# First expert tile in four feature steps: pick, gate product, up product, and half-slot loads

## The chip, the cores and the metric

One core of a Trainium2 chip runs the kernel. The metric is the device time of one execution in microseconds, here the median of several runs. Engines: PE (TensorE), DVE (VectorE), ACT (ScalarE), POOL (GpSimd), SP (SyncE, which here only issues loads).

## What is computed

One decoder layer over 512 tokens of width 2048 in float32: a norm, an input projection, three mixers (attention, S5, HGRN2), an output projection, then a mixture of experts and a final norm. The change lies in the mixture of experts. Cut to what matters:

```
gl = x @ w_group;  g_idx = argmax(gl)                    # 1 of 4 groups
top_vals, top_idx = top_k(el_of_group, 2)                # 2 of 8 experts in it
xs = tokens ordered by expert
h = silu(xs @ w_gate[e]) * (xs @ w_up[e])                # 2048 -> 512
y = h @ w_down[e]                                        # 512 -> 2048
out[token] += gate * y
```

There are 32 experts. Each has 4.2 MB of gate, 4.2 MB of up and 4.2 MB of down weights (float32), and every expert's weights are read once.

## The kernel before, in words

**Tiles and owners.** The experts are worked off in 14 tiles of 128 rows. In a tile the PE array's four column groups of 32 rows each belong to one or more experts. Tile 0 has two experts (`THREE_ONE`: expert 0, fixed at build time, has three groups; the "partner", known only after routing, has one), tile 1 has four (`FOUR`), tiles 2 to 8 two each, tiles 9 to 12 two each, the last one four.

**Parts and slots.** Weights come in parts of 2 MiB (128 partitions x 4096 values): gate half 0, gate half 1, up half 0, up half 1, two for down. Eight slots in SBUF take them. `part` (L783 on) waits until the slot's last reader is done (`slot_used`), then SP issues the load; SP is one queue in order, so a part that waits holds back every part behind it. For tile 0 the parts are numbered 0 to 11 (`fixed_parts`), even ones of expert 0 and odd ones of the partner. Parts 0, 1 are gate half 0; 2, 3 up half 0; 4, 5 gate half 1; 6, 7 up half 1; 8 to 11 down. The partner's parts 5, 7, 9, 11 share their slots with parts 0, 1, 2, 3: part 5 follows part 0, part 7 follows part 1, part 9 follows part 2, part 11 follows part 3. They are loaded in two pieces of 1 MiB: `first_half` (L789) when PE has read the first half of the slot (`half_read`), and `second_half` (L795) when it has read the whole slot (`slot_used`). The order on SP (L831 to L835) is: first pieces of 5 and 7, second pieces of 5 and 7, first pieces of 9 and 11, second pieces of 9 and 11, then tile 1's 24 parts. Tile 1's parts 0 to 3 (gate half 0 of its four experts) go into the slots of tile 0's parts 4, 5, 6 and 7; its parts 4 to 7 go into the slots of tile 0's down parts.

**Tile 0 on PE.** Its rows are picked by products with a 0/1 matrix (`select`): for each quarter f of the features (512 of 2048), 16 products into one bank, which DVE then scales into SBUF (`turned`, one operation each, signalled by `xT_free`). `expert_tile(0, ..., first=True)` does select(0), select(1), then the gate and up products of the first 1024 features (`first_products` with `FIRST_ORDER`: gate half 0, up half 0, gate half 1, up half 1), with the routing's last product `id` between the first two and select(2), select(3) before the third. Each of these four products is 32 calls, 64 instructions in the trace (a call in float32 is two instructions). Before select(0) stands `keep_warm(TURN_BANK[0], 1)` (L1437), one product whose result nobody reads.

**DVE meanwhile** works off the routing: it makes the matrix for `select` (`first_sel`), the order of the experts (`order_ready`, for which SP waits before it can load the partner's parts), the places (`places_ready`, for `id`), then from the result of `id` the token numbers (`slots_ready`), on which POOL gathers tile 1's token rows, 1 MiB, on a DMA queue of its own. `turned` for quarters 0, 1 and for 2, 3 stands at fixed places in this program.

**The other tiles.** `first_products` for tiles 1 on waits for the four `turned` of its tile and for its parts; then come the transposes for the next tile, `hidden_back` and the down products.

## Time and profile before

| | us |
|---|---|
| runs | 1895.19, 1898.34, 1899.38 |
| median | 1898.34 |
| profiled execution | 1895.62 |
| its span in the trace | 1893.8 |
| PE busy | 1773.5 (94%) |
| HBM read | 496.92 MB |
| GB/s in the 40 slices, slices 20 to 39 | 371 to 427 |

The span is the time between the first and the last recorded instruction. A window of the trace gives for a stretch how long each engine was busy, the TensorE clock that was granted (1.00 is 2.4 GHz, 0.50 is 1.2 GHz) and the bytes that the 16 DMA engines moved. A timeline gives instructions in order. "Idle before" is the time in which an engine did nothing ahead of an instruction, with what ended it. The duration of a DMA instruction in SP's timeline is the time to issue it, not to move the data; the list of DMA issues gives the time to landing.

### The profile page before, as it was taken

The numbers are of one execution on the slowest core, as the hardware profiler recorded it, in microseconds if no ns is written. First come the engines' busy times: TensorE is split into PE (matmuls) and PEld (weight loads), VectorE is DVE, ScalarE is ACT, GpSimd is POOL, SyncE is SP. The second block draws the span as 40 slices with busy tenths as digits, with TensorE's granted clock in tenths as the row PEclk, the third lists the DMA queues.
The fourth block names the chain that finished last, engine by engine and source line by source line (L and its number), as shares of the span: only waits on it lengthen the run. The fifth ranks groups of instructions, "written<-read, shape, count | busy, mean of one in ns | idle before, by whom it ended". The sixth has DMA issues, their size and how long they took to land.

```text
span 1893.8 us, 30543 instructions
## 1 busy us (share of the span) xinstructions
PE 1773.5 (94%) x12903; PEld 1088.4 (57%) x12903; DVE 750.8 (40%) x1422; ACT 242.7 (13%) x581; POOL 181.0 (10%) x207
## 2 busy tenths in 40 slices
PE   6999999999999989999987599999999999999985
PEld 4888899878997878888532133332333333333321
DVE  7666685366457543332511112231222322232311
ACT  4012211200325330000100000000000000000021
POOL 1453342000000000000010000000000000000001
PEclk9999999999999999999998799999999999999988
DMA  6343333322112155221989999999999999999997
GB/s 224 104 140 91 101 91 93 100 91 64 60 63 78 51 211 198 73 88 47 374 371 427 426 426 425 425 426 425 426 425 426 426 426 425 426 426 426 419 415 320
DMA packets 67464, 505.74 MB, mean 267 GB/s; under 512 B 18712, under 2 KB 18988, under 8 KB 37688
## 3 DMA queue, kind: packets, MB, share of 16 engines
q1 hardware_dynamic: 47666, 475.85, 62.0%
q0 software_dynamic: 5728, 19.56, 3.0%
q10 hardware_dynamic: 13936, 8.36, 1.8%
q8 instruction: 108, 1.77, 0.4%
q14 instruction: 26, 0.20, 0.0%
HBM read 496.92 MB, written 14.04 MB: 270 GB/s over the span
## 4 chain that ended last, share of the span: by engine, by line
PE 72%; DMA 20%; DVE 3%; ACT 1%; issue 1%; SPq 1%; POOLq 0%; DVEq 0%; ACTq 0%
PE psum L1509 18%; PE psum L1151 16%; DMA arena<-in_moe_w_gate 14%; PE psum L1148 10%; PE psum L1117 10%; PE psum L1465 6%; PE psum L1550 4%; DMA arena<-in_moe_w_up 3%; DMA arena<-in_moe_w_down 2%; PE psum L1217 1%; DVE arena L1978 1%; PE psum L1445 1%; SPq L873 1%; PE psum L1357 1%; DVE arena L1981 1%
## 5 line engine op out<-in xcount | busy, mean ns | idle before, releaser
L1509 PE MATMUL psum<-arena 128*32 128x512 f32 x3584 | 417.7, 620 | 50.5 <-DMA arena<-in_moe_w_gate 21.3
L1978 DVE TENSOR_TENSOR arena<-psum,arena 128x512 f32<-128x512 f32 (+3 forms) x299 | 197.9, 677 | 390.9 <-PE psum L1465 355.5
L1151 PE MATMUL psum<-arena 128*128 128x256 f32 x1456 | 323.2, 381 | 1.2 <-DVE arena L1978 1.2
L1509 PEld LDWEIGHTS psum<-arena 128*32 128x32 f32 x3584 | 119.6, 114 | 340.0 <-issue 335.3
L1151 PEld LDWEIGHTS psum<-arena 128*128 128x128 f32 x1456 | 273.8, 190 | 39.1 <-issue 2.1
L1978 DVE TENSOR_TENSOR arena<-arena,psum 128x256 f32<-128x256 f32 (+1 forms) x143 | 70.4, 492 | 410.3 <-PE psum L1117 124.1
L1148 PE MATMUL psum<-arena 128*128 128x128 f32 x1792 | 205.1, 276 | 0.0
L1148 PEld LDWEIGHTS psum<-arena 128*128 128x128 f32 x1792 | 202.2, 192 | 1.3 <-issue 0.8
L1550 PE MATMUL psum<-arena 128*32 128x512 f32 x1664 | 185.8, 605 | 16.8 <-DMA arena<-in_moe_w_down 16.8
L1117 PE MATMUL psum<-arena 128*128 128x256 f32 x896 | 198.3, 381 | 0.5 <-issue 0.5
L1465 PE MATMUL psum<-arena 128*128 128x512 f32 x416 | 193.6, 609 | 2.3 <-issue 2.3
L1978 DVE TENSOR_TENSOR arena<-arena 128x128 f32<-128x128 f32 (+17 forms) x434 | 175.4, 447 | 31.8 <-ACT arena L1691 24.1
L1117 PEld LDWEIGHTS psum<-arena 128*128 128x128 f32 x896 | 169.4, 191 | 29.2 <-issue 7.3
L1465 PEld LDWEIGHTS psum<-arena 128*128 128x128 f32 x416 | 75.6, 191 | 120.9 <-issue 120.9
L1550 PEld LDWEIGHTS psum<-arena 128*32 128x32 f32 x1664 | 54.3, 112 | 139.0 <-issue 138.0
L656 DVE TENSOR_TENSOR arena<-arena 128x1024 f32<-128x1024 f32 x84 | 109.4, 1302 | 2.3 <-DVE arena L1978 1.1
L1015 POOL TENSOR_SCALAR arena<-arena 128x512 f32<-128x512 f32 x13 | 27.1, 2082 | 727.4 <-PE psum L1465 727.0
L1903 ACT ACTIVATE arena<-psum 128x512 f32<-128x512 f32 x14 | 8.4, 597 | 361.2 <-PE psum L1486 361.2
L1772 ACT ACTIVATE arena<-psum 128x256 f32<-128x256 f32 (+1 forms) x46 | 18.4, 399 | 265.4 <-PE psum L1151 177.5
L1899 ACT ACTIVATE arena<-psum,arena 128x512 f32<-128x512 f32 x14 | 9.6, 687 | 293.6 <-PE psum L1509 227.7
L2621 DVE COPY arena<-psum 128x512 f32<-128x512 f32 x13 | 9.0, 692 | 96.2 <-PE psum L1550 96.2
L2618 DVE COPY arena<-psum 128x512 f32<-128x512 f32 x13 | 9.0, 692 | 85.9 <-PE psum L1550 85.9
(249 smaller groups left out, 1079.4 us busy)
## 6 DMA issues: line engine op xcount, KB each, us to landing
arena<-in_moe_w_gate SPq DMA_DIRECT2D x63, 2048.0 KB, 26.0
arena<-in_moe_w_up SPq DMA_DIRECT2D x63, 2048.0 KB, 24.7
arena<-in_moe_w_down SPq DMA_DIRECT2D x54, 2048.0 KB, 26.5
arena<-in_w_in SPq DMA_DIRECT2D x86, 512.0 KB, 4.6
arena<-in_w_out SPq DMA_DIRECT2D x16, 1024.0 KB, 5.7
arena<-in_moe_w_down SPq DMA_DIRECT2D x12, 1024.0 KB, 15.5
arena<-in_x SPq DMA_DIRECT2D x8, 1024.0 KB, 12.7
arena<-in_moe_w_down SPq DMA_DIRECT2D x16, 512.0 KB, 12.1
```

The lines of the kernel that those rows point to most:

```text
L656: e.tensor_tensor(F(o, BLK), F(a, BLK), F(b, BLK), ALU.subtract).then_inc(sums_ready, 1)
L873: sp.dma_start(dst, src).then_inc(tail_in[p], 16)
L1015: g.tensor_scalar(F(SEL, S), F(IOTA, S), F(SELP, 1), F(SELP + 1, 1), ALU.is_equal, ALU.mult).then_inc(sel_ready, 1)
L1117: last = mm(B(bank, [(1, 2 * P)], off=2 * t * P), F(a + t * P, P), F(w + 2 * i * P, 2 * P), start=(n < 4 and i == 0 and t == 0), stop=(i = ...
L1148: last = mm(B(bank, [(1, P)], off=t * P), F(a + t * P, P), F(w + i * P, P), start=start and t == 0, stop=(i == KH - 1), skip_group_check=True)
L1151: last = mm(B(bank, [(1, HB)]), F(w + i * P, P), F(a, HB), start=start, stop=(i == KH - 1), skip_group_check=True)
L1217: last = mm(B(bank, [(1, S)]), F(w + k * P, P), F(ZT + k * S, S), start=(k == 0), stop=(k == NB5 - 1))
L1357: last = mm(B(bank, [(1, n)]), F(AQ + h * S + i * P, P, m * QK, QK), F(AK + h * S, n, m * QK, QK), start=True, stop=True)
L1465: mm(B(4 + q, [(1, 512)]), F(SEL + t * P, P), F(YSB + q * 512, 512), start=True, stop=True).then_inc(comb_full, 1)
L1509: last = mm(B(bank, [(1, FE)], 32 * g, 32), F(xt + c * CAP + 32 * g, 32), F(SLOT[slot] + (c % 8) * FE, FE), start=(c == 0), stop=(c == KD ...
L1550: last = mm(B(4 + q, [(1, 512)], 32 * g, 32), F(HTE + m * CAP + 32 * g, 32), down_block(slot, m, q), start=(m == 0), stop=(m == FT2 - 1))
L1978: return v.tensor_tensor(o, a, b, op)
```

## The change

Tile 0 gets its own function, `first_tile`. For each quarter f of the features it does select(f), (for f = 1 also `id`), waits for that quarter's `turned`, and does the gate product and the up product of the quarter's 4 chunks. `half_read` is now raised four times: after gate and up of quarter 0, and after gate and up of quarter 2. On SP the orders for parts 5, 7, 9 and 11 stay. New is that tile 1's parts 0 to 3 are loaded in two pieces as well: first pieces when `half_read` reaches 3 (parts 0, 1) and 4 (parts 2, 3), each also behind the landing of the load before it on the same semaphore `half_in`; second pieces when the slot is read. On DVE `turned(0, (0,))` moves behind the place computation, and `turned(0, (1,))` from there to just ahead of the copy of `id`'s result. The `keep_warm` ahead of the picks is gone.

```diff
--- before.py
+++ after.py
@@ -834,9 +834,12 @@
                 for j in two_:
                     second_half(partner, fixed_parts()[j], *FIRST_ORDER[j // 2])
             four, parts = [], four_parts()
-            for j in range(FOUR_L):
-                if j < 4:
-                    four.append(expert(2 + j))
+            for j in range(4):
+                four.append(expert(2 + j))
+                first_half(four[j], parts[j], 0, 0, 3 + j // 2, j % 2)
+            for j in range(4):
+                second_half(four[j], parts[j], 0, 0)
+            for j in range(4, FOUR_L):
                 part(four[j % 4], parts[j], j // 8, j // 4 % 2)
             two_, parts = [expert(6 + i) for i in range(2)], second_parts()
             for j in range(PAIR_L):
@@ -1434,7 +1437,6 @@
 
             for bank in range(8):
                 pe.wait_ge(free[bank], uses[bank] - (bank == use[("id",)][0]))
-            keep_warm(TURN_BANK[0], 1)
 
             def select(fs):
 
@@ -1445,13 +1447,6 @@
                             last = mm(B(TURN_BANK[f], [(1, CAP)], off=c * CAP), F(H0 + t * D + (4 * f + c) * P, P),
                                       F(SB[0] + t * P, P), start=(t == 0), stop=(t == TB - 1))
                     last.then_inc(xT_full, 1)
-
-            def during_first(half):
-
-                if half == 1:
-                    do(("id",))
-                elif half == 2:
-                    select((2, 3))
 
             def combine(m, t):
 
@@ -1486,48 +1481,67 @@
                     last = tr(B(2, [(1, CAP)], off=m * CAP), F(SIL + m * P, P), ident)
                 last.then_inc(hT_full, 1)
 
-            def first_products(n, parts, owner, later, ahead=None, xt=XT):
+            def first_products(n, parts, owner, split):
 
                 ne = max(owner) + 1
-                if xt == XT:
-                    pe.wait_ge(xT_free, 4 * n + 4)
-                for step, (which, half) in enumerate((FIRST_ORDER if xt != XT else ORDER)[:4]):
+                pe.wait_ge(xT_free, 4 * n + 4)
+                if split:
+                    for s in half_in:
+                        pe.wait_ge(s, 16 * 4)
+                for step, (which, half) in enumerate(ORDER[:4]):
                     bank = 2 + which
                     here = parts[step * ne:(step + 1) * ne]
-                    if ahead is not None:
-                        ahead(step)
-                    if xt != XT and step >= 2:
-                        pe.wait_ge(half_in[step - 2], 16)
+                    for slot, before in here:
+                        pe.wait_ge(slot_in[slot], 16 * (before + 1))
                     for c in range(8 * half, 8 * half + 8):
-                        if xt != XT and which == 0 and c % 4 == 0:
-                            pe.wait_ge(xT_free, c // 4 + 1)
-                        if c % 8 == 0:
-                            for slot, before in here:
-                                pe.wait_ge(slot_in[slot], 16 * (before + 1))
                         for g in range(4):
                             slot = here[owner[g]][0]
-                            last = mm(B(bank, [(1, FE)], 32 * g, 32), F(xt + c * CAP + 32 * g, 32),
+                            last = mm(B(bank, [(1, FE)], 32 * g, 32), F(XT + c * CAP + 32 * g, 32),
                                       F(SLOT[slot] + (c % 8) * FE, FE), start=(c == 0), stop=(c == KD - 1))
                             if c % 8 == 7 and last_of_owner(owner, g):
                                 last.then_inc(slot_used[slot], 1)
-                            elif c % 8 == 3 and g == 3 and xt != XT and step < 2:
-                                last.then_inc(half_read, 1)
-                        if c % 8 == 7 and later:
-                            combine(n - 1, step)
+                    yield step
+
+            def first_tile(parts, owner):
+
+                for f in range(4):
+                    select((f,))
+                    if f == 1:
+                        do(("id",))
+                    pe.wait_ge(xT_free, f + 1)
+                    for which in range(2):
+                        step = 2 * (f // 2) + which
+                        here = parts[2 * step:2 * step + 2]
+                        if f == 2:
+                            slot, before = here[0]
+                            pe.wait_ge(slot_in[slot], 16 * (before + 1))
+                            pe.wait_ge(half_in[which], 16)
+                        else:
+                            for slot, before in here:
+                                pe.wait_ge(slot_in[slot], 16 * (before + 1))
+                        for c in range(4 * f, 4 * f + 4):
+                            for g in range(4):
+                                slot = here[owner[g]][0]
+                                last = mm(B(2 + which, [(1, FE)], 32 * g, 32), F(XT0 + c * CAP + 32 * g, 32),
+                                          F(SLOT[slot] + (c % 8) * FE, FE), start=(c == 0), stop=(c == KD - 1))
+                                if c % 8 == 7 and last_of_owner(owner, g):
+                                    last.then_inc(slot_used[slot], 1)
+                        if f % 2 == 0:
+                            last.then_inc(half_read, 1)
 
             def down_block(slot, m, q):
 
                 at_ = SLOT[slot] + q % 2 * D
                 return F(at_ + m * 512, 512) if q < 2 else V(at_ + m * 256, [(1024, 2), (1, 256)])
 
-            def expert_tile(n, par, pair, parts, owner, first=False):
+            def expert_tile(n, par, pair, parts, owner, first=False, split=False):
 
                 ne = max(owner) + 1
                 if first:
-                    select((0, 1))
-                    first_products(n, parts, owner, False, during_first, XT0)
+                    first_tile(parts, owner)
                 else:
-                    first_products(n, parts, owner, True)
+                    for step in first_products(n, parts, owner, split):
+                        combine(n - 1, step)
                 turn(n + 1, 1 - par, pair + par, (0, 1), 16 * n)
                 hidden_back(n)
                 turn(n + 1, 1 - par, pair + par, (2, 3), 16 * n)
@@ -1540,7 +1554,7 @@
                         for slot, before in here:
                             pe.wait_ge(slot_in[slot], 16 * (before + 1))
                         if first:
-                            pe.wait_ge(half_in[q // 2], 32)
+                            pe.wait_ge(half_in[q // 2], 16 * 2)
                     pe.wait_ge(y_act if q % 2 == 0 else y_dve, 2 * n + 1)
                     if q >= 2:
                         pe.wait_ge(xT_free, 4 * n + q + 5)
@@ -1615,7 +1629,10 @@
                         if q == 3:
                             last.then_inc(same_full, 1)
 
-                first_products(n, parts, on_partitions(FOUR), False, ahead)
+                ahead(0)
+                for step in first_products(n, parts, on_partitions(FOUR), False):
+                    if step < 3:
+                        ahead(step + 1)
                 hidden_back(n)
                 pe.wait_ge(hT_done, n + 1)
 
@@ -1650,7 +1667,7 @@
                     same_part(p)
 
             expert_tile(0, 0, 0, fixed_parts(), on_partitions(THREE_ONE), True)
-            expert_tile(1, 1, 0, four_parts(), on_partitions(FOUR))
+            expert_tile(1, 1, 0, four_parts(), on_partitions(FOUR), split=True)
             expert_tile(2, 0, 1, second_parts(), on_partitions(THREE_ONE))
             with pe.Fori(2, 1 + (A_END - 1) // 2) as it:
                 for k in range(2):
@@ -2540,7 +2557,6 @@
             dve.wait_ge(h_rst, 1)
             diffs = V(RGD, [(5, TB), (1, 5)])
             tt(diffs, diffs, V(RST, [(1, TB), (0, 5)]), M).then_inc(diffs_ready, 1)
-            turned(0, (0,), XT0)
             settle(tt(V(RTMP, all3), rk, V(RCP, [(0, TB), (1, NE)]), ALU.is_ge))
             put(tt(V(RTMP, all3), V(RTMP, all3), V(ROB, [(0, TB), (1, NE)]), M))
             settle(tt(V(REL, all3), rk, V(RBS, [(0, TB), (1, NE)]), AD))
@@ -2549,7 +2565,7 @@
                 settle(tt(F(RTMP, 128), F(oh, 128), F(REL, 128), M))
                 settle(v.tensor_reduce(F(RPF + k * TB, TB), V(RTMP, all3), AX.X, AD))
 
-            turned(0, (1,), XT0)
+            turned(0, (0,), XT0)
             dve.wait_ge(exps_ready, 1)
             second = V(RGE + NGRP, [(5, TB)])
             settle(v.tensor_reduce(F(RGS, TB), V(RGE, [(5, TB), (1, NGRP)]), AX.X, AD))
@@ -2578,6 +2594,7 @@
             settle(ts(F(REI, NOV), F(REI, NOV), float(NE - 1), None, ALU.min))
             settle(v.tensor_copy(F(REI + NOV, 1), F(RCU + NE - 1, 1)))
             settle(v.tensor_copy(F(EID, NOV + 1).bitcast(I32), F(REI, NOV + 1)))
+            turned(0, (1,), XT0)
             s = ("id",)
             bank = see_bank(dve, s)
             got = B(bank, [(1, NT)], 0, CAP)
```

## Rows read from the trace of the kernel before

**Rows 1.** The page's chain that ended last, by engine.

```profile
PE 72%; DMA 20%; DVE 3%; ACT 1%; issue 1%; SPq 1%; POOLq 0%; DVEq 0%; ACTq 0%
```

**Rows 2.** Windows: span, PE, PEld, DVE, ACT, POOL busy; PEclk, DMA share, GB/s.

```profile
1000.00:1050.00 50.00, 29.55 (x159) 9.11 (x161) 8.30 (x12) 0.69 (x1) 0.00 (x0) 0.81 1.01 426
...
1500.00:1550.00 50.00, 48.82 (x367) 17.32 (x365) 13.33 (x21) 2.57 (x5) 3.64 (x5) 1.00 1.01 427
```

**Rows 3.** The same columns in stretches of 4 us around tile 0.

```profile
932.00:936.00 4.00, 4.00 (x40) 1.17 (x36) 3.73 (x15) 0.00 (x0) 0.00 (x0) 1.00 0.35 147
936.00:940.00 4.00, 4.00 (x39) 1.92 (x32) 3.32 (x9) 0.00 (x0) 0.00 (x0) 1.00 0.86 301
...
944.00:948.00 4.00, 4.00 (x38) 1.23 (x31) 0.00 (x0) 0.00 (x0) 0.58 (x1) 1.00 1.01 418
...
956.00:960.00 4.00, 4.00 (x44) 1.21 (x40) 0.00 (x0) 0.00 (x0) 0.00 (x0) 1.00 0.48 201
960.00:964.00 4.00, 4.00 (x40) 1.17 (x36) 0.00 (x0) 1.76 (x2) 0.00 (x0) 1.00 0.30 61
964.00:968.00 4.00, 4.00 (x44) 1.25 (x40) 0.00 (x0) 0.21 (x1) 0.00 (x0) 1.00 0.94 397
```

**Rows 4.** Timeline of SP: start, duration, line, load and count.

```profile
921.68 0.35 SPq L787 DMA_DIRECT2D arena<-in_moe_w_gate  x1
922.13 0.38 SPq L787 DMA_DIRECT2D arena<-in_moe_w_up  x1
935.56 0.33 SPq L793 DMA_DIRECT2D arena<-in_moe_w_gate  x1
...
938.98 0.33 SPq L798 DMA_DIRECT2D arena<-in_moe_w_gate  x1
...
962.29 23.94 SPq L787 DMA_DIRECT2D arena<-in_moe_w_gate  x8
```

**Rows 5.** DMA issues at 921.7, 922.1, 935.6 us: KB each, us to landing.

```profile
arena<-in_moe_w_gate SPq DMA_DIRECT2D x1, 2048.0 KB, 9.3
...
arena<-in_moe_w_up SPq DMA_DIRECT2D x1, 2048.0 KB, 13.7
...
arena<-in_moe_w_gate SPq DMA_DIRECT2D x1, 1024.0 KB, 4.8
```

**Rows 6.** Timeline of PE: start, duration, line, operation, count, [idle before].

```profile
921.88 2.02 PE L1159 MATMUL psum<-arena 128*128 128x512 f32 x2 [1.00 <-DVE arena L2514]
923.70 8.10 PE L1445 MATMUL psum<-arena 128*128 128x128 f32 x64
931.73 7.07 PE L1509 MATMUL psum<-arena 128*32 128x512 f32 x64
938.73 2.02 PE L1426 MATMUL psum<-arena 128*128 128x90 f32 x16
...
947.68 7.41 PE L1445 MATMUL psum<-arena 128*128 128x128 f32 x64
955.03 13.94 PE L1509 MATMUL psum<-arena 128*32 128x512 f32 x128
...
971.26 13.94 PE L1550 MATMUL psum<-arena 128*32 128x512 f32 x128
```

**Rows 7.** Timeline of DVE, the first `turned` and the work behind it.

```profile
928.26 0.69 DVE L1978 TENSOR_TENSOR arena<-psum,arena 128x512 f32<-128x512 f32 x1 [2.51 <-PE psum L1445]
928.87 1.46 DVE L1978 TENSOR_TENSOR arena<-arena 128x128 f32<-128x128 f32 x5
```

**Rows 8.** Timeline of POOL, the first gather of token rows.

```profile
943.48 1.09 POOL L1004 DMA_INDIRECT arena<-hs_rows,arena  x1 [0.95 <-POOL arena L1001]
```

**Rows 9.** Windows of 1 us at the routing's end, columns as Rows 2.

```profile
922.00:923.00 1.00, 1.00 (x2) 0.33 (x2) 0.93 (x6) 0.00 (x0) 0.00 (x0) 0.50 1.33 451
...
925.00:926.00 1.00, 1.00 (x9) 1.00 (x9) 0.65 (x4) 0.22 (x1) 0.00 (x0) 0.83 0.89 377
```

**Rows 10.** Timeline of PE in the last tile, a product behind one DVE operation.

```profile
1848.53 0.66 PE L1486 MATMUL psum<-arena 128*128 128x128 f32 x4 [0.86 <-DVE arena L1978]
```

## The prediction

> **What bounds the kernel now.** I read the page's chain first. It puts 72% on PE and 20% on DMA [rows 1], which averages two different stretches, so the next view is the table of windows. Up to about 985 us the PE order sets the time. Behind it the weights do: in the window from 1000 us PE is busy for 29.55 of 50 us while DMA stands at a share of 1.01 and 426 GB/s, and 500 us later it is still 427 GB/s, with PE now at 48.82 of 50 [rows 2]. In the expert stretch the time is therefore bytes over 426 GB/s, plus every microsecond in which the DMA engines stand idle before the stream becomes unbroken. That moment lies in tile 0, and the third view to read is the short windows there. At 426 GB/s a window of 4 us is full. The windows from 932 and 936 us lack (426 - 147)/426 x 4 = 2.6 us and 1.2 us; those from 956, 960 and 964 us lack 2.1, 3.4 and 0.3 us [rows 3]. So there are two holes, **A of 3.8 us** and **B of 5.8 us**, 9.6 us in all. PE is fully busy through both [rows 3], yet PE time alone is worth nothing here: tile 1 waits for its gate parts, and the weights already set the pace from 990 us. What counts is when PE releases a load. The question for the change is what it does to A + B.
>
> Hole A is the wait of parts 5 and 7 for the first half of their slots: their load is issued at 935.56 [rows 4], after half of the gate product that begins at 931.73 [rows 6]. Hole B is the wait of tile 1's first parts for the third product: issued at 962.29 [rows 4], halfway through the 13.94 us that begin at 955.03 [rows 6].
>
> **The change on PE, step by step.** (1) Without the unread product (L1159, 2.02 us, from 921.88 to 923.9) select(0) could begin some 0.5 us sooner, at about 923.2, when its matrix is ready. But the clock is at half at that point (0.50 at 922, 0.83 over 925 to 926, so it rises at about 925.3) [rows 9], and the work that brings it up again, which began at 921.88, now begins at 923.2. If the rise comes as long after the beginning as before, 3.4 us, it comes at 926.6, and select(0), 3.7 us of work at full clock (7.41/2 [rows 6]), ends at 926.6 + 3.7 - 1.7 = 928.6 instead of 928.2. This is a loss of 0.4 us, not a gain of 0.5, but step 2 hides it either way.
>
> (2) `turned` of quarter 0 is moved behind five more DVE operations and two passes of reduction, which stand behind it at 928.87 and now fill the 2.51 us in which DVE idled [rows 7]; it ends at about 929.4. The gate product of quarter 0 also needs part 1, the partner's, issued at 921.68 and landing 9.3 us later, at 931.0 [rows 4, 5]. So it runs from **931.1 to 934.7** (half of 7.07 us [rows 6]). The up product behind it needs part 3: issued at 922.13 with 13.7 us to landing, 935.8 [rows 4, 5]. In the kernel before that product began at 940.7 and never met this wait. So it runs from **935.9 to 939.4**. PE has lost time here that nothing hides: two waits for the partner's parts, 2.5 and 1.2 us.
>
> (3) Then select(1) 3.7, `id` 2.0 (its `turned` of quarter 1 lies under it) and the gate product of quarter 1, 3.5 us: it ends at 948.7. Up to **952.2**. select(2) 3.7, and now a bare wait for `turned`: nothing stands between the pick and its use. The nearest row is a product behind one DVE operation of this size, 0.86 us of idle [rows 10]; the lower bound is 0.69 us, the operation itself [rows 7]; I take 0.9. Gate and up of quarter 2 end at 960.3 and **963.9**. select(3), 0.9, gate and up again: 972.0 and **975.5**, where the kernel before was at 968.9. The down products move from 971.3 to about 977.9 and end at 991.8 instead of 985.2 [rows 6].
>
> **The change on the load queue.** A 1 MiB piece is 2.46 us at 426 GB/s. A load that finds the queue empty brings the rate back about 1.6 us after its issue (hole A ends at 933.4 + 3.8 = 937.2, issue 935.56) [rows 3, 4]. The lack in the window from 932 us puts the queue's end at 933.4.
> - *Hole A.* First pieces of 5 and 7 go out at 934.7 + 0.3 = 935.0, so the rate is back at 936.6: 3.2 us, where it was 3.8. Gain 0.6.
> - *Hole B'.* Those two pieces are through at 941.5. Next on SP stand the second pieces of 5 and 7, and they wait until the whole slot is read, which is the gate product of quarter 1: 948.7 + 0.3 = 949.0 instead of 938.98 [rows 4]. In between PE has up(0), select(1), `id` and gate(1), 14 us, where it had half a product. The first pieces of 9 and 11 have been free since 939.4, but SP is one queue and they stand behind. So the engines idle from 941.5 to 949.0 + 1.6 = 950.6, 9.1 us, less what the gather of tile 1's rows moves on its own queue. It was issued at 943.48, 2.7 us after `id` ended at 940.7 [rows 6, 8]; now `id` ends at 945.1, the gather goes out at about 947.9 and moves from about 949.8. **Hole B' is 8.3 us**, between 8.0 and 9.1.
> - *Hole B.* Behind 950.6 the queue holds the second pieces of 5 and 7, the first of 9 and 11, and from 952.5 their second ones, 6 MiB and 1 MiB of gather: full until 967.6. Tile 1's first pieces 0 and 1 are released by the gate product of quarter 2 (960.3) and by landings at about 961 and 963.5: early enough. Hole B (5.8 us) is **gone**. Pieces 2 and 3 wait for the landings of pieces 0 and 1, at about 971 and 973.4, with one other piece in flight each time; against 4.8 us from issue to landing for a lone piece [rows 5] this leaves 0 to 2.5 us of idle in each of two places. I take 0.5 for both together, since the rate needs 1.6 us to start and 2.46 us of work is still queued. Second pieces 0 to 3 follow at 973 to 976, with gathers 2 and 3 (2 MiB), until 992. Parts 4 and 5 are released by the second down product at 985, so there is no hole there.
> - *Sum.* Before: 3.8 + 5.8 = 9.6. After: 3.2 + 8.3 + 0.5 = 12.0. If the clock falls in the waits of step 2, at 928.6 to 931.1 PE is as idle as it was before the fall at 922, and a spell at half clock costs 1.7 us of PE (3.4 us at half). Of that only what ends after part 3's landing counts: a gate product at half clock ends at 936.3 instead of 934.7, 0.4 us past 935.9. I add 0.4: 12.4, or **+2.8**. Four more pieces of 1 MiB in place of 2 MiB parts: the window from 944 us, in which only such pieces and the gather ran, shows 418 GB/s against 426 [rows 2, 3], 2% of 8 MiB, +0.3. Together **+3.1 us**.
>
> The Trainium skill ("DMA: Bandwidth & Descriptors", section "Bandwidth", its measured table) speaks against the change more strongly: it gives 341 GB/s, 78% of the peak, for a single 1 MB transfer. By that rule the 8 MiB of tile 1 that now go in eight pieces would take 24.6 us rather than 19.7, and the sum would be about +7.7 us. The row from 944 us, 418 GB/s from pieces queued behind one another, does not agree, so it enters as a rival only, below in terms of this kernel.
>
> From the profiled execution's own time 1895.62 the sum gives 1898.7; it lies 2.7 us below the median of the runs, and set against that, 1898.34, it gives **1901.4 us**. The span moves from 1893.8 to about 1896.9.
>
> **The rivals.** *(R1) The halves drain the queue; slower.* Pieces 2 and 3 of tile 1 wait for landings of 0 and 1, and 0 and 1 for those of 9 and 11. If the queue runs dry each time, a piece costs 4.8 us from issue to landing instead of 2.46 of transfer [rows 5], 2.3 us for each of two steps beyond my 0.5: +4.2, in all +7.3 or 1905.6. It decides from the point at which PE's third product ends later than about 966, so that the queue of 7 MiB is used up before piece 0 is out. For it: each wait is real. Against it: seven MiB stand ahead. The same time comes out if the clock falls between 936 and 949, where 1.7 us of PE go straight into hole B' and again into the pieces of tile 1. Chance 0.22.
>
> *(R2) Part 3 is not what PE waits for.* If gate(0) could begin at 929.5 and up(0) at 933.0, hole A is 1.5, the two pieces are through at 939.8, gate(1) ends at 945.7, B' is 6.8 less a little, and the sum is 8.8 against 9.6: about -0.5 with the smaller pieces, 1897.8. For it: `turned` is done at 929.4. Against it: the two landing times. Chance 0.13.
>
> *(R3) The hole does close: faster.* It needs B' to be no more than some 2 us, that is, the pieces of 9 and 11 moving while 5 and 7 wait. The order on SP would have to be another, or the rate after 966 us would not be what sets the end, so that earlier landings of tile 1 (its first pieces at 970 instead of 971 to 974) let PE finish ahead. The unbroken 426 GB/s [rows 2] speaks against it. It would give -5.8 + 0.6 + 0.3 or about 1893. Chance 0.07.
>
> *(R4) The stream swallows it.* If the DMA engines had slack later (a rate of 426 with PE at 48.8 of 50 [rows 2] may partly be PE's pace), the 6.6 us that PE loses in tile 0 would count in part and the 2.8 us of idle not: between 0 and +6.6. I count this with the forecast's width.
>
> **How the numbers follow.** Forecast +1.5 to +4.5: 0.58, R1 0.22, R2 0.13, R3 0.07. The range goes from R2's lower edge, 1896.5, to 1906.5, with R1 inside; what is left out is most of R3 and the far end of R1. What a measurement of this kernel can tell from no change is about 0.2%, 3.8 us: from 1894.5 to 1902.1 is the same. The forecast, 1901.4, lies just inside, with 0.16 of its 0.58 beyond. Slower: R1 plus that, 0.37. Faster: 0.08. Same: 0.55.
>
> **What would show each step.** The up product of quarter 0 beginning at 935.9 behind a DMA wait on part 3 (step 2); the second piece of part 5 issued at 949 rather than 939, and windows near 0 GB/s from 942 to 949 (B'); no window under 300 GB/s between 951 and 985 (B gone; a dip near 972 is R1); tile 0's down products ending at 991 to 992; tile 1's first product beginning near 993 instead of 990.2. A second piece of 5 issued before 945 would make the forecast wrong, as would a rate below 420 GB/s behind 1000 us.

## The result, and the profile after

The changed kernel takes 1900.30 us, the median of 18 runs, where the kernel before takes 1896.87 us in 18 runs beside them. The ratio is 1.0015, with a 95% interval from 1.0009 to 1.0022: **2.8 us slower, between 1.7 and 4.2** (the medians alone differ by 3.4). The profiled execution took 1901.03 us with a span of 1899.1, against 1895.62 and 1893.8.

The windows of 4 us of the changed kernel (columns as in Rows 2) are the lines to set beside [rows 3]:

```profile
932.00:936.00 4.00, 3.22 (x32) 0.94 (x24) 3.71 (x9) 0.00 (x0) 0.00 (x0) 1.00 0.37 156
936.00:940.00 4.00, 3.53 (x32) 1.13 (x32) 1.23 (x5) 0.00 (x0) 0.00 (x0) 1.00 0.90 328
940.00:944.00 4.00, 4.00 (x39) 3.96 (x36) 0.01 (x1) 0.00 (x0) 0.00 (x0) 1.00 0.49 201
944.00:948.00 4.00, 4.00 (x39) 2.28 (x42) 1.75 (x7) 0.20 (x1) 0.19 (x1) 1.00 0.00 0
948.00:952.00 4.00, 4.00 (x40) 1.17 (x36) 0.00 (x0) 0.00 (x0) 1.10 (x1) 1.00 0.48 131
...
956.00:960.00 4.00, 3.22 (x32) 1.15 (x34) 0.69 (x1) 0.00 (x0) 0.00 (x0) 1.00 1.01 426
...
968.00:972.00 4.00, 3.22 (x33) 1.07 (x36) 0.69 (x1) 0.00 (x0) 0.00 (x0) 1.00 0.88 360
972.00:976.00 4.00, 4.00 (x42) 1.09 (x31) 0.02 (x1) 1.97 (x2) 0.00 (x0) 1.00 0.96 336
```

Hole B of the kernel before (956 to 968 in [rows 3]) is gone: 426 GB/s at 956. In its place stands one from 940 to 952, in the middle of which not a byte moves: 0 GB/s in every window of 1 us from 943 to 950. From windows of 1 us, each lacking (426 - GB/s)/426, the holes are 3.4 (A), 8.9 (B') and 1.3 us (at 971 to 974), where the kernel before had 3.7 and 5.8. The lack of all windows from 928 to 1010 us added up is **13.8 us against 9.8**. This sum is called the stream's idle time below. It comes from one execution of each kernel. PE stays between 3.22 and 4.00 of 4 us in every line, so its busy share doesn't show the hole.

The loads say why. SP's timeline of the changed kernel, with [rows 4] as its counterpart:

```profile
922.06 0.35 SPq L787 DMA_DIRECT2D arena<-in_moe_w_gate  x1
...
935.41 0.33 SPq L793 DMA_DIRECT2D arena<-in_moe_w_gate  x1
...
949.38 0.33 SPq L798 DMA_DIRECT2D arena<-in_moe_w_gate  x1
...
950.36 0.89 SPq L793 DMA_DIRECT2D arena<-in_moe_w_down  x2
...
961.03 12.89 SPq L793 DMA_DIRECT2D arena<-in_moe_w_gate  x4
974.11 2.84 SPq L798 DMA_DIRECT2D arena<-in_moe_w_gate  x4
```

The first pieces of 5 and 7 go out at 935.4, as before. The second ones go out at 949.38 instead of 938.98, and the first pieces of parts 9 and 11 right behind them, at 950.36, though PE had read their half by 940.1. In the kernel before they went out here:

```profile
944.38 0.89 SPq L793 DMA_DIRECT2D arena<-in_moe_w_down  x2
```

PE's timeline of the changed kernel, beside [rows 6]:

```profile
924.29 5.17 PE L1447 MATMUL psum<-arena 128*128 128x128 f32 x32 [2.43 <-DVE arena L1998]
931.58 3.64 PE L1525 MATMUL psum<-arena 128*32 128x512 f32 x32 [2.12 <-DMA arena<-in_moe_w_gate]
936.47 3.64 PE L1525 MATMUL psum<-arena 128*32 128x512 f32 x32 [1.25 <-DMA arena<-in_moe_w_up]
940.04 3.84 PE L1447 MATMUL psum<-arena 128*128 128x128 f32 x32
943.72 1.92 PE L1429 MATMUL psum<-arena 128*128 128x90 f32 x16
945.57 7.07 PE L1525 MATMUL psum<-arena 128*32 128x512 f32 x64
...
957.19 7.07 PE L1525 MATMUL psum<-arena 128*32 128x512 f32 x64 [0.78 <-DVE arena L1995]
...
978.18 13.94 PE L1564 MATMUL psum<-arena 128*32 128x512 f32 x128
994.30 6.20 PE L1499 MATMUL psum<-arena 128*32 128x512 f32 x40 [2.18 <-DMA arena<-in_moe_w_gate]
```

The bracket at the end of a line is the idle time ahead of it. PE waits 2.12 us for part 1, 1.25 us for part 3, then does up(0), select(1) and `id`, and the gate product of quarter 1 (the first half of the 7.07 us from 945.57) ends at 949.1. Tile 0's down products begin at 978.18, 6.9 us later than in [rows 6]. Tile 1's first product begins at 994.30, where it was 990.21.

The span grew by 5.3 us, more than the runs did. PE's timeline at the end, first of the kernel before and then of the changed one, shows the difference:

```profile
1879.16 1.93 PE L1634 MATMUL psum<-arena 128*32 128x256 f32 x32 [1.89 <-DMA arena<-in_moe_w_down]
```

```profile
1882.80 3.62 PE L1651 MATMUL psum<-arena 128*32 128x256 f32 x32 [1.88 <-DMA arena<-in_moe_w_down]
```

The last product of the down weights starts 3.6 us later. That much is the stream. The other 1.7 us is its duration, 3.62 instead of 1.93 us: this execution met it at half clock, as its window of 1 us shows:

```profile
1883.00:1884.00 1.00, 1.00 (x12) 0.43 (x8) 0.00 (x0) 0.00 (x0) 0.77 (x1) 0.50 0.98 393
```

The change isn't what does that: e3_pe_late (2.86 us) and e6_small_pieces (3.27 us) below, with PE's order of before in tile 0, have a long last product too, and e2_whole_parts, with the changed order, has 1.93.

Behind 1000 us the stream is as full as before: in windows of 50 us up to 1750 both kernels have 425 to 427 GB/s. The two windows from there to 1850 have 421 and 419 GB/s, and 419 and 415 in the kernel before. The prediction named a rate below 420 behind 1000 us as a sign that would make it wrong. Taken by the letter that sign appears, but it appears at the end of both kernels and so says nothing of the change.

### The profile page after: what moved, and what is told of

It reads as the page before. It is cut to its first block, busy times and chain, and to the rows that moved or that the text cites. A ratio compares the mean times of both kernels' runs of the same rounds, so it can differ in the third digit from the quotient of the medians.

```text
span 1899.1 us, 30558 instructions
## 1 busy us (share of the span) xinstructions
PE 1770.0 (93%) x12901; PEld 1086.2 (57%) x12901; DVE 751.1 (40%) x1422; ACT 243.0 (13%) x581; POOL 181.3 (10%) x207
## 4 chain that ended last, share of the span: by engine, by line
PE 73%; DMA 20%; DVE 3%; ACT 1%; SPq 1%; issue 1%; POOLq 0%; DVEq 0%; ACTq 0%
PE psum L1499 17%; PE psum L1154 16%; DMA arena<-in_moe_w_gate 14%; PE psum L1151 10%; PE psum L1120 10%; PE psum L1460 6%; DMA arena<-in_moe_w_up 4%; PE psum L1564 3%; DMA arena<-in_moe_w_down 2%; PE psum L1525 1%; PE psum L1220 1%; DVE arena L1995 1%; SPq L876 1%; PE psum L1447 1%; PE psum L1360 1%
## 5 line engine op out<-in xcount | busy, mean ns | idle before, releaser
L1499 PE MATMUL psum<-arena 128*32 128x512 f32 x3328 | 385.3, 617 | 52.2 <-DMA arena<-in_moe_w_up 22.4
L1499 PEld LDWEIGHTS psum<-arena 128*32 128x32 f32 x3328 | 109.7, 113 | 322.4 <-issue 317.6
L1564 PE MATMUL psum<-arena 128*32 128x512 f32 x1664 | 185.3, 603 | 17.4 <-DMA arena<-in_moe_w_down 17.4
L1564 PEld LDWEIGHTS psum<-arena 128*32 128x32 f32 x1664 | 54.2, 111 | 139.1 <-issue 138.1
```

The source lines that it names most:

```text
L1499: last = mm(B(bank, [(1, FE)], 32 * g, 32), F(XT + c * CAP + 32 * g, 32), F(SLOT[slot] + (c % 8) * FE, FE), start=(c == 0), stop=(c == KD ...
L1564: last = mm(B(4 + q, [(1, 512)], 32 * g, 32), F(HTE + m * CAP + 32 * g, 32), down_block(slot, m, q), start=(m == 0), stop=(m == FT2 - 1))
```

## The experiments

**Theory H**: the end is set by when the bytes are through, so each change counts by what it does to the stream's idle time, whatever PE does in tile 0. **Rival P**: it is PE's later end of tile 0 that counts. **Rival S**: pieces of 1 MiB are slow in themselves. Each kernel ran beside the kernel before on the same chip: the change 18 times, e2 and e9 5 times, the others 11 times. The microseconds are the ratio of the runs times 1897. "Idle time" and the third column are read from one execution each.

| kernel | idle time of the stream, 928 to 1010 us | tile 0's down products begin | ratio to before (95%) | us |
|---|---|---|---|---|
| before | 9.8 | 971.3 | | 0 |
| the change | 13.8 | 978.2 | 1.0015 (1.0009 to 1.0022) | +2.8 |
| e1_pieces_first | 11.3 | 979.5 | 1.0005 (0.9996 to 1.0014) | +1.0 |
| e2_whole_parts | 19.4 | 977.8 | 1.0056 (1.0042 to 1.0069) | +10.6 |
| e3_pe_late | 10.1 | 975.7 | 1.0000 (0.9991 to 1.0009) | 0.0 |
| e4_before_split | 6.3 | 971.4 | 0.9989 (0.9980 to 0.9998) | -2.1 |
| e5_hybrid | 10.2 | 973.6 | 1.0005 (0.9996 to 1.0014) | +1.0 |
| e6_small_pieces | 11.3 | 972.0 | 1.0002 (0.9993 to 1.0011) | +0.4 |
| e7_unread_back | 12.9 | 977.0 | 1.0015 (1.0006 to 1.0024) | +2.8 |
| e8_hybrid_order | 6.5 | 973.3 | 0.9984 (0.9975 to 0.9993) | -3.0 |
| e9_held_load | 17.1 | 971.5 | 1.0039 (1.0025 to 1.0053) | +7.4 |

### The two theories apart: PE late without a hole, a hole without a late PE

e3_pe_late, on the kernel before:

```diff
                 if first:
                     once_copied(("id",))
+                    pe.wait_ge(y_act, 1)
+                    keep_warm(4, 7)
```

> The kernel before with seven unread products of 512 columns (14 instructions, about 6.5 us at full clock) ahead of tile 0's down products. They end tile 0 on PE as late as the change does, and leave the loads of tile 0 and of tile 1's parts 0 to 3 where they were. Theory H: parts 4 and 5 of tile 1 are released at about 985 instead of 978.4, while the queue is full until 990: no hole, 0 us (-1 to +1). Rival P: +3 to +6.5 us.

PE's timeline of e3_pe_late has the unread products and the down products behind them:

```profile
969.51 6.25 PE L1159 MATMUL psum<-arena 128*128 128x512 f32 x14
975.70 13.94 PE L1552 MATMUL psum<-arena 128*32 128x512 f32 x128
```

Everything on this execution's clock lies 1.7 us early (the third product pair begins at 953.4, not 955.0), so PE is 6.1 us late at the down products. The time is the same: 0.0 us, between -1.7 and +1.7. Rival P's 3 to 6.5 us is excluded.

e9_held_load, on the kernel before:

```diff
+            sp.wait_ge(slot_used[SD], 2)
             for j in range(FOUR_L):
                 if j < 4:
                     four.append(expert(2 + j))
```

> The kernel before, with tile 1's first load held until the slot of tile 0's part 6 is read out (968.9) instead of that of part 4 (962.3). No product and no other engine's work changes in tile 0; only hole B grows by 6.6 us. Theory H (idle time of the DMA engines counts in full): +6 to +7 us. Rival P: 0 to +1, since PE's products of tile 0 stay where they are. Rival D (the stream has slack behind 1000 us that swallows part of a hole): +2 to +4.

Windows and SP's timeline of e9_held_load:

```profile
956.00:960.00 4.00, 4.00 (x42) 1.18 (x37) 0.04 (x1) 0.00 (x0) 0.00 (x0) 1.00 0.54 225
960.00:964.00 4.00, 4.00 (x44) 1.29 (x40) 0.00 (x0) 1.54 (x2) 0.00 (x0) 1.00 0.00 0
964.00:968.00 4.00, 4.00 (x44) 1.17 (x36) 0.00 (x0) 0.43 (x1) 0.00 (x0) 1.00 0.01 4
968.00:972.00 4.00, 4.00 (x40) 2.50 (x36) 2.72 (x5) 0.60 (x1) 0.78 (x2) 1.00 0.35 70
```

```profile
969.96 16.50 SPq L787 DMA_DIRECT2D arena<-in_moe_w_gate  x8
```

```profile
955.25 13.94 PE L1510 MATMUL psum<-arena 128*32 128x512 f32 x128
...
971.48 13.94 PE L1551 MATMUL psum<-arena 128*32 128x512 f32 x128
```

PE's products lie where they lay, 971.48 against 971.26. The stream's idle time is 7.3 us longer, and the run 7.4 us (4.7 to 10.0). A hole ahead of the unbroken stream counts in full as far as this interval tells. Rival D, that later slack swallows part of it (R4 of the prediction; +2 to +4), is excluded.

One rival no run separates: that what counts is the start of PE's first product of tile 1, which waits for the same loads. It moves nearly as the stream does (990.21 before, 997.71 in e9). Against it stands only an argument from the windows: in the 100 us from 1000 on PE is busy for 62.8 us in the kernel before and for 61.6 us in the changed one, while the DMA rate is 426 to 427 GB/s in both, so PE has some 37 us in which to make up a late start, and the stream has none.

### The two halves of the change

e2_whole_parts, on the changed kernel, takes back the early release of tile 1's loads:

```diff
-            for j in range(4):
-                four.append(expert(2 + j))
-                first_half(four[j], parts[j], 0, 0, 3 + j // 2, j % 2)
-            for j in range(4):
-                second_half(four[j], parts[j], 0, 0)
-            for j in range(4, FOUR_L):
+            for j in range(FOUR_L):
+                if j < 4:
+                    four.append(expert(2 + j))
                 part(four[j % 4], parts[j], j // 8, j // 4 % 2)
...
-            expert_tile(1, 1, 0, four_parts(), on_partitions(FOUR), split=True)
+            expert_tile(1, 1, 0, four_parts(), on_partitions(FOUR))
```

> The changed kernel with tile 1's first four parts loaded whole, 2 MiB each, once their slots are read out, as in the kernel before; PE's order is that of the change. It takes away the half of the change that releases loads earlier. Theory H: hole B' stays (8 to 9 us) and a second hole of 5.5 to 7.5 us opens behind 968, where the queue is empty and the gate product of quarter 3 has not ended: +7 to +10 us against the kernel before. Rival P: PE's order is the same as in the change, so +2.8. Rival S: fewer small pieces, so +2.8 or less.

Windows of e2_whole_parts:

```profile
964.00:968.00 4.00, 3.67 (x32) 3.48 (x32) 0.29 (x1) 0.00 (x0) 0.00 (x0) 1.00 0.52 213
968.00:972.00 4.00, 3.54 (x36) 1.16 (x40) 0.40 (x1) 0.00 (x0) 0.00 (x0) 1.00 0.01 4
972.00:976.00 4.00, 4.00 (x41) 1.36 (x34) 0.38 (x1) 1.97 (x2) 0.00 (x0) 1.00 0.69 233
```

A second hole of 7.8 us, from 965 to 975, stands behind B', which has 7.9 us in this kernel. The cost is 10.6 us (8.0 to 13.1), a little over the +7 to +10 expected, with PE's order that of the change. So the new order of the products, with the moved `turned` on DVE and without the unread product, is worth +10.6, and the early pieces of tile 1 give 7.8 of it back. Rival P (+2.8 here) and rival S (+2.8 or less) are excluded.

e4_before_split, on the kernel before, is the other half alone:

```diff
-            for j in range(FOUR_L):
-                if j < 4:
-                    four.append(expert(2 + j))
+            for j in range(4):
+                four.append(expert(2 + j))
+            for k in (0, 2):
+                for j in (k, k + 1):
+                    first_half(four[j], parts[j], 0, 0, 3 + k // 2, j % 2)
+                for j in (k, k + 1):
+                    second_half(four[j], parts[j], 0, 0)
+            for j in range(4, FOUR_L):
                 part(four[j % 4], parts[j], j // 8, j // 4 % 2)
...
-                            elif c % 8 == 3 and g == 3 and xt != XT and step < 2:
+                            elif c % 8 == 3 and g == 3 and xt != XT:
                                 last.then_inc(half_read, 1)
```

(Tile 1's products also wait for the pieces, as in the change.)

> The kernel before, PE's order unchanged, with the other half of the change alone: half_read is also raised in the middle of the third and fourth product of tile 0, and tile 1's parts 0 to 3 go in two pieces each, in the order first 0, 1, second 0, 1, first 2, 3, second 2, 3. Theory H: tile 1's first piece goes out at about 958.9 instead of 962.3, hole B falls from 5.8 to about 2.5 us, and no other hole opens: -2 to -3.5 us against the kernel before. Rival P: PE is not touched in tile 0, so 0. Rival S: 0 to +5.

Windows and SP's timeline of e4_before_split, against the 201 and 61 GB/s of [rows 3]:

```profile
956.00:960.00 4.00, 4.00 (x44) 1.30 (x40) 0.00 (x0) 0.00 (x0) 0.00 (x0) 1.00 0.61 223
960.00:964.00 4.00, 4.00 (x44) 1.17 (x37) 0.00 (x0) 1.66 (x2) 0.00 (x0) 1.00 0.91 348
```

```profile
958.97 0.91 SPq L793 DMA_DIRECT2D arena<-in_moe_w_gate  x2
962.38 0.85 SPq L798 DMA_DIRECT2D arena<-in_moe_w_gate  x2
```

Hole B falls from 5.8 to 2.5 us and nothing else opens. The kernel is 2.1 us faster than before (0.4 to 3.8), where its idle time says 3.5.

### What in the new order costs: SP's queue

e1_pieces_first, on the changed kernel:

```diff
             for reads, two_ in ((1, (5, 7)), (2, (9, 11))):
                 for i, j in enumerate(two_):
                     first_half(partner, fixed_parts()[j], *FIRST_ORDER[j // 2], reads, i)
-                for j in two_:
-                    second_half(partner, fixed_parts()[j], *FIRST_ORDER[j // 2])
+            for j in (5, 7, 9, 11):
+                second_half(partner, fixed_parts()[j], *FIRST_ORDER[j // 2])
```

> The changed kernel with one edit on SP: the first pieces of parts 9 and 11 are issued ahead of the second pieces of 5 and 7. PE, DVE and the data are the same. Theory H (the time is set by the idle time of the DMA engines before the stream becomes unbroken; the change opened hole B' because SP is one queue): two more pieces, 2 x 2.46 us, move in the hole of 8 to 9 us ahead of the second product of tile 0; some of it comes back as idle time behind 965 us, because the queue is 2 MiB shorter there and tile 1's second pieces wait for the last products. 2 to 4.5 us less than the changed kernel, that is -1.5 to +1 us against the kernel before. Rival P (PE's own later end of tile 0, 6.9 us in the trace, is what counts): as the changed kernel, +2.8 us. Rival S (1 MiB pieces are slow in themselves): as the changed kernel, +2.8.

Windows of e1_pieces_first (this execution is about 1.3 us later than the change's in tile 0):

```profile
944.00:948.00 4.00, 4.00 (x39) 3.21 (x42) 1.57 (x6) 0.00 (x0) 0.00 (x0) 1.00 0.99 401
948.00:952.00 4.00, 4.00 (x40) 1.17 (x36) 0.18 (x1) 0.20 (x1) 1.28 (x2) 1.00 0.37 94
...
960.00:964.00 4.00, 4.00 (x41) 1.17 (x36) 0.00 (x0) 0.00 (x0) 0.00 (x0) 1.00 0.91 324
964.00:968.00 4.00, 4.00 (x38) 2.75 (x31) 0.00 (x0) 0.00 (x0) 0.00 (x0) 1.00 0.89 311
```

B' shrinks from 8.9 to 3.5 us, 5.4 us for two pieces of 2.46. But at 962 to 971 there are 2.5 us of new gaps, where the change had only the dip of 1.3 us, and another 1.0 us is lost from 987 to 991, where tile 1's next loads go out at 987.10: the queue is 2 MiB shorter there. Of 5.4 us gained, 2.5 are left in the stream's idle time. The run is 1.0 us over the kernel before, the upper edge of what I expected, with an interval (-0.8 to +2.7) that overlaps the change's 1.7 to 4.2. The trace shows the mechanism; the times alone don't separate the two.

e7_unread_back, on the changed kernel, puts `keep_warm(TURN_BANK[0], 1)` back ahead of the picks.

> The changed kernel with the unread product put back ahead of the picks. Theory H: the clock rises about 1.3 us earlier and select(0) takes less, but the gate product of quarter 0 waits for the landing of part 1 either way: as the changed kernel, +2.8 us against before (+1.8 to +3.8). Rival C (the unread product hides a spell at half clock that the change pays for): 0.9 to 1.9 us less than the changed kernel.

PE's timeline of e7_unread_back:

```profile
923.65 4.68 PE L1449 MATMUL psum<-arena 128*128 128x128 f32 x32
930.41 3.64 PE L1527 MATMUL psum<-arena 128*32 128x512 f32 x32 [2.08 <-DMA arena<-in_moe_w_gate]
```

select(0) takes 4.68 instead of 5.17 us, and the gate product still waits 2.08 us for part 1 (2.12 in the change). The time is +2.8 us (1.1 to 4.6), as the change. The interval doesn't exclude rival C's far end (+1.9); the trace decides against it. In this execution the removed product costs nothing because the partner's load ends last. The cover is thin: in e2_whole_parts select(0) took 6.72 us, more of it at half clock, and there the gate product waited for `turned` (0.85 us) and not for part 1.

e6_small_pieces, on the kernel before, issues tile 1's parts 0 to 3 as two pieces each, but both behind the wait for the whole slot:

```diff
+                for j in (k, k + 1):
+                    sp.wait_ge(slot_used[parts[j][0]], parts[j][1] + 1)
+                    sp.wait_ge(half_in[j % 2], 16 * (2 + k // 2))
+                    sp.dma_start(F(SLOT[parts[j][0]], 2048),
+                                 half_of_expert(four[j], 0, 0)[:, :2048]).then_inc(half_in[j % 2], 16)
```

> The kernel before with tile 1's parts 0 to 3 in two pieces of 1 MiB each, both issued only when the slot is read out, so that no load is released earlier. It measures what the smaller pieces cost by themselves. Theory H: 418 GB/s against 426 over 8 MiB, +0.3 us (-0.7 to +1.3). Rival S: four more pieces with their own start and a lower rate, +5 us.

It took +0.4 us, between -1.3 and +2.1. Rival S's 5 us is excluded. The 0.3 us that I expected can't be told from nothing. Its stream idled 11.3 us, but the extra 1.5 us lies in hole A (5.1 us in this execution), ahead of any piece of tile 1, so it isn't the edit's.

### A version from both kernels

e5_hybrid keeps quarters 0 and 1 as in the kernel before, so that the second pieces of 5 and 7 are free at 939, and takes the change's single steps for quarters 2 and 3, so that tile 1's first pieces are free at 956, before the queue is empty at 958. The core of the edit, on the kernel before:

```diff
-                elif half == 2:
-                    select((2, 3))
...
+            def last_quarters(parts, owner):
+
+                for f in (2, 3):
+                    select((f,))
+                    pe.wait_ge(xT_free, f + 1)
+                    for which in range(2):
...
+                        if f == 2:
+                            last.then_inc(half_read, 1)
```

> Quarters 0 and 1 as in the kernel before (picks 0 and 1 together, gate and up over 1024 features, the unread product kept), quarters 2 and 3 as in the change (pick, wait, gate, up), with tile 1's parts 0 to 3 in pieces in the order first 0, 1, second 0, 1, first 2, 3, second 2, 3. Theory H: the second pieces of 5 and 7 are released as early as in the kernel before, and the first pieces of tile 1 at about 956, before the queue is empty at 958, so hole B closes and A stays; some 1 to 2 us of idle open near 968. -2.5 to -5 us against the kernel before. Rival P: PE ends tile 0 about 2 us later than before: 0 to +2. Rival S: 0 to +5.

It did not come out: +1.0 us (-0.8 to +2.7) where I expected -2.5 to -5. The number speaks for rival P (0 to +2), the trace doesn't. SP's timeline and one window of e5_hybrid:

```profile
956.45 2.01 SPq L793 DMA_DIRECT2D arena<-in_moe_w_gate  x2
968.05 0.85 SPq L798 DMA_DIRECT2D arena<-in_moe_w_gate  x2
969.13 1.01 SPq L793 DMA_DIRECT2D arena<-in_moe_w_gate  x2
```

```profile
964.00:968.00 4.00, 3.77 (x36) 1.20 (x40) 0.17 (x1) 0.00 (x1) 0.00 (x0) 1.00 0.12 47
```

Hole B all but closed (0.9 us from 958 to 962), but from 963 to 970 the stream idled 5.4 us. I had taken over e4's order on SP (first 0, 1, second 0, 1, first 2, 3). The second pieces 0 and 1 are free only at 968, and the first pieces 2 and 3, free at 959.6, stood behind them. This is the trap of hole B' a second time. e8_hybrid_order changes only this:

```diff
-            for k in (0, 2):
-                for j in (k, k + 1):
-                    first_half(four[j], parts[j], 0, 0, 3 + k // 2, j % 2)
-                for j in (k, k + 1):
-                    second_half(four[j], parts[j], 0, 0)
+            for j in range(4):
+                first_half(four[j], parts[j], 0, 0, 3 + j // 2, j % 2)
+            for j in range(4):
+                second_half(four[j], parts[j], 0, 0)
```

> The hybrid again (quarters 0 and 1 as before, 2 and 3 in single steps), with one edit on SP: the order of tile 1's pieces is first 0, 1, 2, 3, then second 0, 1, 2, 3, as in the change. In the hybrid's trace the engines stood for 5.4 us from 963 to 970, because the first pieces 2 and 3, free at 959.6, stood on SP behind the second pieces 0 and 1, free at 968. Theory H: that hole shrinks by the two pieces, 4.9 us: -2.5 to -4.5 us against the kernel before, about 4 us under the hybrid. Rival P (PE ends tile 0 2.3 us later than before): 0 to +2, as the hybrid.

The same two views of e8_hybrid_order:

```profile
956.17 10.02 SPq L793 DMA_DIRECT2D arena<-in_moe_w_gate  x4
967.77 4.33 SPq L798 DMA_DIRECT2D arena<-in_moe_w_gate  x4
```

```profile
964.00:968.00 4.00, 4.00 (x40) 1.28 (x44) 0.00 (x0) 0.28 (x1) 0.00 (x0) 1.00 0.92 328
```

328 GB/s stand where the hybrid had 47, the idle time falls from 10.2 to 6.5 us, and the kernel takes 3.0 us less than before (1.3 to 4.7), with PE's order that of the hybrid. It has the lowest ratio of all versions, though e4_before_split (0.4 to 3.8 us less than before) isn't clear of it. Nothing on PE differs between the last two kernels and their intervals against the kernel before don't meet (-0.8 to +2.7, -4.7 to -1.3), so the 4 us between them are SP's order alone. Rival P, under which both take the same time, is excluded.

## Why the prediction was right, point by point

**The sum.** I forecast +3.1 us and it is +2.8 (1.7 to 4.2). As a time that was 1901.4 us, from a median of three runs that lay 1.5 us over that of 18; measured are 1900.30. The reason held: the end follows the stream's idle time and not PE. e3 (PE 6.1 us late, 0.0) and e9 (PE in place, 7.3 us of idle, +7.4) show the two separately, and in the table no kernel's time is more than 1.4 us from what its idle time says. Closer than that the two can't be compared: hole A alone, which e6 doesn't touch, was 3.7 us in one execution and 5.1 in another.

**Waits for the partner's parts.** Forecast: gate(0) at 931.1, up(0) at 935.9. Trace: 931.58 and 936.47, both behind a DMA wait. Of the half microsecond, 0.4 lies ahead: part 1's load went out at 922.06 in this execution, not 921.68. Step 1 held as well: select(0) took 5.17 us, 5.4 by the forecast, with the granted clock at 0.50 in the windows from 924 to 927.

**PE's later steps.** Forecast: down products of tile 0 from 977.9 to 991.8, tile 1's first product near 993. Trace: 978.18 to 992.12, and 994.30. The waits for `turned` of quarters 2 and 3 are 0.78 us each, where I took 0.9.

**Hole A.** Forecast 3.2, trace 3.4 us (3.8 by the 4 us windows before, 3.7 by those of 1 us).

**Hole B'.** Forecast 8.3, trace 8.9 us. The piece went out at 949.38 (forecast 949.0). The mis-sized term is the gather. POOL's timeline of the changed kernel:

```profile
948.31 1.10 POOL L1007 DMA_INDIRECT arena<-hs_rows,arena  x1 [0.95 <-POOL arena L1004]
```

It was issued 0.4 us later than I said, and the windows of 1 us show 0 GB/s up to 950:

```profile
949.00:950.00 1.00, 1.00 (x16) 0.38 (x12) 0.00 (x0) 0.00 (x0) 0.41 (x1) 1.00 0.00 0
```

So it moved nothing ahead of the pieces that can be seen, where I had credited it with 0.8 us. Without that credit the forecast's hole is 9.1 us.

**Hole B and the pieces' own waits.** B is gone, as forecast. For the waits of pieces 2 and 3 on landings I took 0.5 us; the trace has 1.3 us at 971 to 974 (360 and 336 GB/s in the windows from 968 and 972). That is the mechanism of rival R1 at a fifth of its price: piece 0 landed 9.9 us after 961.03, at 970.9, just as the queue ran out. e8 has the same hole, 1.5 us at 963 to 966.

**The clock.** I added 0.4 us for a fall to half clock in PE's waits for parts 1 and 3. It didn't fall in them. Windows of 1 us of the changed kernel, in the 2.12 us wait and in the 1.25 us one:

```profile
930.00:931.00 1.00, 0.00 (x0) 0.00 (x0) 0.90 (x6) 0.00 (x0) 0.00 (x0) 1.00 0.92 393
...
935.00:936.00 1.00, 0.22 (x4) 0.00 (x0) 0.78 (x3) 0.00 (x0) 0.00 (x0) 1.00 0.04 16
```

So three terms were off: hole B' by +0.6, the waits on landings by +0.8 and the clock by -0.4 us. They don't cancel: by the trace the idle time grew by 4.0 us, 0.9 more than the forecast. That the runs gave +2.8, only 0.3 us from the forecast, is partly luck. What is shown is an effect of 1.7 to 4.2 us, which holds both numbers.

**The unread product.** Forecast: hidden by part 1's landing whichever way it goes. e7 shows it: the gate product waits about 2.1 us for part 1 with it or without it.

**The pieces' size.** The estimate by the Trainium skill ("DMA: Bandwidth & Descriptors", section "Bandwidth") was +7.7 us in all, 4.9 of it for the eight pieces. e6 measures +0.4 (-1.3 to +2.1) for the same eight pieces. The page's 78% of the peak, measured per transfer issued from GpSimd, doesn't carry over to pieces that are queued behind one another on SP: here they cost nothing that can be measured.

**R2, R3, R4.** The wait for part 3 was there, so R2 is out for this execution. R4 is out by e9. R3's sum (-5.8 + 0.6 + 0.3) enters the 0.6 us gained at hole A with the wrong sign; it should be -6.1. R3 named the order on SP as what stood between the change and a gain. e1 shows that the order alone doesn't bring it back for the changed kernel (+1.0, -0.8 to +2.7), since the queue runs short later. e8 shows that it does once the second pieces of 5 and 7 are free early as well.

## What to carry to other kernels

When a stream of loads sets the end, cost an edit on PE by the moments at which it releases loads, and not by PE's time: list for each load when its buffer is free and what stands ahead of it on the issuing queue. A finer release is worth something only if the queue issues in the order of the releases; a piece that is free early behind one that is free late gains nothing (4 us between e5_hybrid and e8_hybrid_order). A hole that is closed early comes back in part where the queue is then shorter (e1: 5.4 us closed, 2.5 left).

## What the runs showed of the hardware that I had not expected

A wait of 2.12 us and, 3.6 us behind its end, one of 1.25 us left TensorE at full clock (1.00 in both windows above), and the same pair of waits in e7_unread_back (2.08 and 1.25 us) did too: the gate and up products behind them take 3.64 us each, half of 7.07. In the kernel before the clock stood at 0.50 at 922 [rows 9] behind 1.00 us of idle [rows 6]. The last product of the down weights shows it most plainly: behind waits of 1.89 and 1.88 us it took 1.93 us in the kernel before and 3.62 us, at 0.50, in the changed one. The length of the idle time just ahead of a product doesn't tell by itself whether the clock falls. What does decide it, no run here shows.
